# A two-block fp32 transformer kernel: token-tile entries with wide up and gate products, and pooling factors moved into the band matrix and the weights

## The chip, the cores and the metric

The kernel runs on one core of one Trainium2 chip. The metric is the device time of one execution in microseconds (us); less is better. Engines are named as in the profile: PE is TensorE's matmul stream, PEld its weight loads, DVE is VectorE, ACT is ScalarE, POOL is GpSimd, SP is SyncE, which issues the weight transfers.

## What is computed

Two blocks of two layers each on 256 tokens of width 1024, all in float32. Block one: causal attention, a squared-ReLU MLP, a pooling mixer, a second MLP. Block two: latent attention, a SwiGLU layer (called ffn here), shared keys and values, chunked attention, a second ffn. The parts that the change touches, cut from the reference:

```python
def pool_mixer(xn, w_groups, ls_scale):
    ...                      # per group: trailing mean over 2, 4, 8 or 16 tokens, minus the token
    y = jnp.einsum('bsgc,gcd->bsgd', pooled.astype(xn.dtype), w_groups)
    return y.reshape(b, s, D_MODEL) * ls_scale

def squared_relu_mlp(x, w_up, w_down):
    h = jax.nn.relu(x @ w_up)
    return (h * h) @ w_down

def swiglu(h, w_gate, w_up, w_down):
    return (jax.nn.silu(h @ w_gate) * (h @ w_up)) @ w_down

# second block, each layer
x = x + rms_norm_2(y, attn_post_g[layer])
h = rms_norm_2(x, ffn_pre_g[layer])
f = swiglu(h, ffn_w_gate[layer], ffn_w_up[layer], ffn_w_down[layer])
x = x + rms_norm_2(f, ffn_post_g[layer])
```

## The kernel before

**Numbers in two parts.** A float32 operand is used as a high part (rounded to the fast matmul format fp32r) plus a low part (the rest). `product` makes each matrix product from three matmuls into the same sums: high by high, low by high, high by low. Weights come in 1 MB chunks `raw[slot]` of 128 x 2048, four slots; ACT writes the high part `whi` (`hi_part`, L611), DVE the low part `wlo` (`lo_part`, L964), in the order of the chunk list, and PE waits for a chunk with `wait_chunk`. SP refills `raw` once the low part is made. `hi_before(c)` and `lo_before(c)` put into ACT's and DVE's queues the parts of all chunks whose slot is free before chunk c.

**Up and gate chunks.** `tiles_out` takes a chunk of 1024 x 256 weights as stationary 128 x 128 tiles and streams the 256 tokens of `act_hi` or `act_lo`: 2 output tiles x 8 input tiles x 3 matmuls of 256 columns, 48 in all. In an MLP ACT then takes the ReLU, DVE squares (L1210), ACT makes `hhi`, DVE `hlo`. In an ffn DVE scales the gate by the token's norm (L1238), ACT takes silu, DVE multiplies by the up product (L1246). The two MLPs have 16 up chunks each, the two ffns 11 gate and 11 up chunks each; the key part of the shared keys and values has 4 chunks of the same shape.

**Down chunks.** `rows_out` keeps token tiles stationary and streams 512 weight columns: 24 matmuls into four banks, one for each quarter (half of the width, token tile). PE's order is up(i+1), down(i), so the hidden tile i has one up chunk (an ffn: a gate and an up chunk) of time to be made ready.

**Entries.** Between two layers the sums in the four banks become the next layer's input. In block two `post` does this on DVE: ACT sums squares of a whole token tile from the banks (L642), DVE multiplies by the gain row (L1118), makes the inverse root with five small steps, adds to `x` in halves (L1122) and multiplies by the next gain (L1076). PE transposes the four quarters (`turn`, L1608), ACT and DVE make `act_hi` (L664) and `act_lo` (L1091), and the first gate chunk starts when the four parts are there. The norm itself is not yet in this input: its factor for each token is made meanwhile (`stats`, `diagonals`), spread by a small matmul (`spread_scales`) and multiplied in by L1238. These entries are called post0 (into ffn0), fpost0 (into the shared keys) and post1 (into ffn1). `keep_busy` puts dummy matmuls of a constant (L1592) into waits of PE, by the table `BUSY`.

**The pooling entry.** After MLP 0 `residual` adds the quarters to `x` (L1103), `norm("mix1")` waits for ACT's sums over both token tiles and scales `x` by factor and gain (L1031), PE multiplies with the banded matrix `const` (L1898, L1900; `C_BAND`) in plain float32, ACT and DVE split the result (L1349), PE multiplies with the pool weights (L1570 to L1572), and for each quarter DVE multiplies by the row `pool_scale` (L1357), adds to `x` (L1358) and multiplies by the next gain (L1076). Then the transposes, and MLP 1.

**POOL** loads the gain rows (three row slots, freed in turn by DVE) and scales the bias tables of the last attention (L501).

## Time and profile before

| what | value |
|---|---|
| median of 3 runs | 1159.61 us (1159.13 to 1159.83) |
| the profiled execution: its own time | 1158.01 us |
| its span in the trace | 1156.2 us |
| PE busy | 1113.8 us, 96% of the span, 7094 matmuls |
| DVE busy | 676.5 us, 59% |
| ACT busy | 532.0 us, 46% |
| POOL busy | 43.1 us, 4% |
| mean TensorE clock granted | 0.995 of full speed |
| chain that ended last | PE 85%, DVE 9%, ACT 3% |
| transfers | 196.36 MB, mean 170 GB/s |

The time of one run is what the runs are compared by; the span leaves out 1.8 us around it. A matmul's duration in the trace holds its latency, so two that follow each other overlap: what a stream of matmuls costs is read from the distance of their starts. Times within the trace are counted from the start of the span.

### The profile page before, as it was taken

The page shows a single profiled execution, that of the slowest core. Times are in us where ns is not written, and L with a number is a line of the kernel's source. Part 1 is how long each engine was busy: PE and PEld are TensorE (multiplying, and loading weights), DVE is VectorE, ACT ScalarE, POOL GpSimd, SP SyncE. Part 2 cuts the span into 40 slices and gives each one's busy share as a digit, 9 for nine tenths or more (in the row PEclk, how much of TensorE's full clock was granted, in tenths as well). Part 3 has the DMA queues.
Part 4 walks back from the last instruction along what each step waited for, and adds up shares of the span by engine and source line. Part 5 has one row for each costly group of instructions (what it writes and reads, how often), then busy time and mean ns, then how long its engine had stood idle before and what let it go on. Part 6 is the DMA issues. An engine that isn't in the chain of part 4 may idle for free.

```text
span 1156.2 us, 17758 instructions
## 1 busy us (share of the span) xinstructions
PE 1113.8 (96%) x7094; PEld 996.7 (86%) x7094; DVE 676.5 (59%) x941; ACT 532.0 (46%) x645; POOL 43.1 (4%) x71
## 2 busy tenths in 40 slices
PE   7999999999999999998999999999999979999997
PEld 6888899999889999988777999999798759999996
DVE  5756645454665454576667555454955766555554
ACT  5556434434344444345474433434534654334342
POOL 1000000000000000000000000001500410000000
PEclk9999999999999999999999999999999999999999
DMA  9843465555534555554432655556565143555650
GB/s 344 316 147 109 130 214 165 200 183 179 196 108 159 205 178 185 192 135 165 146 110 73 212 188 175 188 181 223 173 218 169 43 132 111 182 183 180 186 177 36
DMA packets 127273, 196.36 MB, mean 170 GB/s; under 512 B 6960, under 2 KB 97200, under 8 KB 127104
## 3 DMA queue, kind: packets, MB, share of 16 engines
q1 hardware_dynamic: 123872, 185.77, 49.0%
q0 software_dynamic: 3216, 9.51, 2.8%
q8 instruction: 27, 0.44, 0.2%
q10 hardware_dynamic: 144, 0.52, 0.1%
q14 instruction: 14, 0.11, 0.0%
HBM read 194.73 MB, written 1.05 MB: 169 GB/s over the span
## 4 chain that ended last, share of the span: by engine, by line
PE 85%; DVE 9%; ACT 3%; issue 1%; DMA 1%; DVEq 0%; SPq 0%; ACTq 0%
PE ps L1570 27%; PE ps L1572 26%; PE ps L1571 26%; DVE wlo L964 2%; DVE xs L1076 1%; ACT whi L611 1%; PE ps L1686 1%; DVE act_lo L1091 1%; DVE x L1122 1%; PE ps L2020 1%; DVE xs L1118 1%; DMA x<-x_in 1%; ACT junk L642 1%; PE ps L2018 1%; PE ps L1712 1%
## 5 line engine op out<-in xcount | busy, mean ns | idle before, releaser
L964 DVE TENSOR_TENSOR wlo<-raw,whi 128x2048 fp32r<-128x2048 f32 (+2 forms) x172 | 386.6, 2266 | 171.2 <-ACT whi L611 170.4
L1570 PE MATMUL ps<-act_hi,whi 128*128 128x256 f32 x1384 | 392.7, 284 | 6.2 <-DVE act_lo L1091 4.0
L1571 PE MATMUL ps<-act_lo,whi 128*128 128x256 f32 x1384 | 391.6, 283 | 0.0
L1572 PE MATMUL ps<-act_hi,wlo 128*128 128x256 f32 x1384 | 391.6, 283 | 0.0
L611 ACT ACTIVATE whi<-raw 128x2048 fp32r<-128x2048 f32 (+2 forms) x171 | 319.5, 1888 | 95.6 <-PE ps L1572 92.0
L1570 PEld LDWEIGHTS ps<-act_hi,whi 128*128 128x128 f32 x1384 | 263.6, 190 | 11.4 <-issue 7.6
L1571 PEld LDWEIGHTS ps<-act_lo,whi 128*128 128x128 f32 x1384 | 263.6, 190 | 2.0
L1572 PEld LDWEIGHTS ps<-act_hi,wlo 128*128 128x128 f32 x1384 | 263.6, 190 | 0.0
L1572 PE MATMUL ps<-whi,hlo 128*128 128x512 f32 x400 | 156.8, 392 | 0.0
L1571 PE MATMUL ps<-wlo,hhi 128*128 128x512 f32 x400 | 156.8, 392 | 0.0
L1570 PE MATMUL ps<-whi,hhi 128*128 128x512 f32 x400 | 156.2, 390 | 0.0
L1570 PE MATMUL ps<-whi,act_hi 128*128 128x512 f32 (+2 forms) x286 | 111.4, 390 | 5.8 <-DVE act_lo L1167 2.5
L1572 PE MATMUL ps<-whi,act_lo 128*128 128x512 f32 (+2 forms) x286 | 107.9, 377 | 0.0
L1571 PE MATMUL ps<-wlo,act_hi 128*128 128x512 f32 (+2 forms) x286 | 107.5, 376 | 0.0
L1210 DVE TENSOR_TENSOR arena<-arena 128x512 f32<-128x512 f32 x32 | 22.1, 692 | 129.1 <-ACT arena L721 129.1
L721 ACT ACTIVATE arena<-ps 128x512 f32<-128x512 f32 x32 | 19.1, 598 | 153.8 <-PE ps L1572 153.8
L1572 PEld LDWEIGHTS ps<-whi,hlo 128*128 128x128 f32 x400 | 75.2, 188 | 16.0
L1570 PEld LDWEIGHTS ps<-whi,hhi 128*128 128x128 f32 x400 | 75.2, 188 | 14.7
L1571 PEld LDWEIGHTS ps<-wlo,hhi 128*128 128x128 f32 x400 | 75.1, 188 | 14.6
L1570 PEld LDWEIGHTS ps<-whi,act_hi 128*128 128x128 f32 x286 | 53.8, 188 | 15.3 <-DVE act_lo L1167 3.2
L1572 PEld LDWEIGHTS ps<-whi,act_lo 128*128 128x128 f32 x286 | 53.7, 188 | 9.8
L1571 PEld LDWEIGHTS ps<-wlo,act_hi 128*128 128x128 f32 x286 | 53.9, 189 | 8.1
(186 smaller groups left out, 873.0 us busy)
## 6 DMA issues: line engine op xcount, KB each, us to landing
raw<-mlp_w_up_in SPq DMA_DIRECT2D x32, 1024.0 KB, 6.4
raw<-mlp_w_down_in SPq DMA_DIRECT2D x32, 1024.0 KB, 4.9
raw<-ffn_w_gate_in SPq DMA_DIRECT2D x22, 1024.0 KB, 5.3
raw<-ffn_w_up_in SPq DMA_DIRECT2D x22, 1024.0 KB, 5.3
raw<-ffn_w_down_in SPq DMA_DIRECT2D x22, 1024.0 KB, 4.8
raw<-attn_w_qkv_in SPq DMA_DIRECT2D x11, 1024.0 KB, 10.9
raw<-w_kv_shared_in SPq DMA_DIRECT2D x8, 1024.0 KB, 6.4
raw<-attn_w_o_in SPq DMA_DIRECT2D x4, 1024.0 KB, 5.1
```

The source lines that it names most:

```text
L611: nc.scalar.activation(whi[:, s, 0:width], raw[:, s, 0:width], ACT.Copy).then_inc(hi_ready, 1)
L642: nc.scalar.activation(junk[:, col * HALF:col * HALF + width], src, ACT.Square, accum_out=norm_stat(name, t, 0, col, col + 1)).then_inc(sq ...
L721: nc.scalar.activation(relu, bank(5 if first else 4), ACT.Relu).then_inc(f.act_done, 1)
L964: nc.vector.tensor_tensor(wlo[:, s, 0:width], raw[:, s, 0:width], whi[:, s, 0:width].bitcast(F32), ALU.subtract).then_inc(lo_ready, 1)
L1076: nc.vector.tensor_tensor(xs[:, t, cols], x[:, t, cols], row(name)[:, cols], ALU.mult)\
L1091: nc.vector.tensor_tensor(act_quarter(act_lo, name, p), bank(4 + p).rearrange("p (k t) -> p k t", t=P), act_quarter(act_hi, name, p).bitca ...
L1118: nc.vector.tensor_tensor(xs[:, t, :], ps[:, t * D:(t + 1) * D], row(name), ALU.mult)
L1122: nc.vector.scalar_tensor_tensor(out=x[:, t, cols], in0=xs[:, t, cols], scalar=norm_stat(name, t, 6), in1=x[:, t, cols], op0=ALU.mult, op1 ...
L1210: nc.vector.tensor_tensor(hf, relu, relu, ALU.mult).then_inc(f.h_done, 1)
L1570: nc.tensor.matmul(dst, lhsT=left[0], rhs=right[0], start=start, stop=False, **kw)
L1571: nc.tensor.matmul(dst, lhsT=left[0], rhs=right[1], start=False, stop=False, **kw)
L1572: return nc.tensor.matmul(dst, lhsT=left[1], rhs=right[0], start=False, stop=stop, **kw)
```

## The change

**Wide products.** `act_hi` and `act_lo` become the two halves of one tile `act`, so that for each 128-row piece the 256 high and 256 low columns lie side by side. `wide_out` replaces `tiles_out` for all up, gate and shared-key chunks: one matmul streams 512 columns against the high weights, and one of 256 columns streams the high activations against the low weights, 32 matmuls for a chunk instead of 48. The high-by-high and low-by-high sums now lie apart in a bank, and each chunk takes two banks; ACT copies the low half out (`copy_rest`), DVE adds the other half (`sum_gate`, `sum_up`, the first step of `square`). ReLU and square are one DVE instruction.

**Entries by token tiles.** At post0, fpost0 and post1 `post_entry` takes the place of `post`. POOL multiplies `x` and the two gain rows ahead of time (`premix_x`, `premix_rows`; 9 instructions of 128 x 1024); DVE makes the next input directly from the banks, token tile 0 before token tile 1; `enter_by_tiles` makes the first chunk's products of tile 0 before tile 1 is transposed. `x` itself is brought up to date later by `update_x`, between the layer's first steps. The dummy matmuls of these entries are gone.

**Pooling.** The token factor of `mix1` goes into the band matrix (`band`, scaled by ACT for token tile 0 and by DVE for tile 1), `pool_scale` into the pool weights (`scale_pool_weights`, one DVE instruction of 128 x 2048 during the last steps of MLP 0). The sums of squares are taken in quarters, MLP 0 ends tile by tile, and the 15 dummy matmuls before the band products and 8 of the 11 after them are gone.

```diff
-                    "fpre0": (4, 1, 6, 1, 2), "kvsrc": (8, 1, 6, 1, 2), 
-                    "fpre1": (4, 1, 6, 1, 2),
...
+            def wide_out(w, b, enter=None):
...
+                        nc.tensor.matmul(bank(b + f), lhsT=w[0][:, at:at + P],
+                                         rhs=act[:, k, :, :].rearrange("p a t -> p (a t)"),
+                                         start=k == 0, stop=False, skip_group_check=True)
+                        ins = nc.tensor.matmul(bank(b + f, 0, T), lhsT=w[1][:, at:at + P], rhs=act_hi[:, k, :],
+                                               start=False, stop=k == KT - 1, skip_group_check=True)
...
+            def enter_by_tiles(name, w, b):
+                turn(name, parts=(0, 1))
+                for t in range(TT):
+                    for kh in range(2):
+                        wait_acts(name, 2 * t + kh + 1)
...
+                                nc.tensor.matmul(both, lhsT=w[0][:, at:at + P], rhs=act[:, k, :, t * P:(t + 1) * P],
+                                                 start=k == 0, stop=False, skip_group_check=True)
+                                ins = nc.tensor.matmul(main, lhsT=w[1][:, at:at + P],
...
+                    if t == 0:
+                        turn(name, parts=(2, 3))
...
                 def gate_up(c, i, value, first=False, spread=False):
...
                     if first:
+                        enter_by_tiles(norm, slot(c), GATE).then_inc(w_used, 1)
+                    else:
+                        pe.wait_ge(f.summed, i * 2 - 1)
+                        wide_out(slot(c), GATE).then_inc(w_used, 1)
...
+                def copy_rest(value, b):
+                    act.wait_ge(w_used, value)
+                    nc.scalar.activation(by_token(up_sum), wide(b)[1], ACT.Copy).then_inc(f.rest_copied, 1)
...
+                    nc.vector.tensor_tensor(by_token(up_sum), wide(b)[0], by_token(up_sum), ALU.add)\
+                        .then_inc(f.summed, 1)
+                    dve.wait_ge(f.summed, i + 1)
+                    nc.vector.scalar_tensor_tensor(out=hf, in0=up_sum, scalar=0.0, in1=up_sum, op0=ALU.max,
+                                                   op1=ALU.mult).then_inc(f.h_done, 1)
...
-            keep_busy(15, 7)
...
+                pe.wait_ge(band_second if t else band_first, 1)
```

DVE's queue at post0, before: from the first statistics of token tile 0 (`stat`) to the low parts of the input.

```order
L1001 TENSOR_SCALAR stat<-stat 128x1
L1118 TENSOR_TENSOR xs<-ps,rows 128x1024
L1017 RECIPROCAL stat<-stat 128x1
...
L1122 SCALAR_TENSOR_TENSOR x<-xs,stat,x 128x512
L1076 TENSOR_TENSOR xs<-x,rows 128x512
L1122 SCALAR_TENSOR_TENSOR x<-xs,stat,x 128x512
L1076 TENSOR_TENSOR xs<-x,rows 128x512
```

This stands twice, once for each token tile, and then come all four low parts. In the changed kernel the same place reads as follows for tile 1 and behind it.

```order
L1238 TENSOR_SCALAR stat<-stat 128x1
L1234 TENSOR_TENSOR arena<-ps,xs 128x512
L1243 SCALAR_TENSOR_TENSOR stat<-stat 128x1
L1198 TENSOR_TENSOR act<-ps,act 128x4x128
L1234 TENSOR_TENSOR arena<-ps,xs 128x512
...
L1198 TENSOR_TENSOR act<-ps,act 128x4x128
L1262 SCALAR_TENSOR_TENSOR xs<-arena,stat 128x512 x2
L1198 TENSOR_TENSOR act<-ps,act 128x4x128 x2
L1071 TENSOR_TENSOR wlo<-raw,whi 128x2048
L1290 TENSOR_TENSOR arena<-ps,rows 128x512 x2
L1294 SCALAR_TENSOR_TENSOR x<-arena,stat,x 128x512 x2
```

The low parts of tile 0 (the first two L1198) moved ahead of tile 1's input (L1262), and the update of `x` (L1290, L1294) moved behind all four.

PE's queue in an up chunk, before, three matmuls of 256 columns for each pair of tiles:

```order
L1570 MATMUL ps<-act_hi,whi 128x256
L1571 MATMUL ps<-act_lo,whi 128x256
L1572 MATMUL ps<-act_hi,wlo 128x256
L1570 MATMUL ps<-act_hi,whi 128x256
L1571 MATMUL ps<-act_lo,whi 128x256
```

The same chunk in the changed kernel, here the first of MLP 1:

```order
L1925 MATMUL ps<-act,whi 128x512
L1928 MATMUL ps<-act,wlo 128x256
L1925 MATMUL ps<-act,whi 128x512
L1928 MATMUL ps<-act,wlo 128x256
L1925 MATMUL ps<-act,whi 128x512
```

One matmul in three is gone, the columns streamed are the same.

## Rows read from the trace of the kernel before

**Rows 1.** The page: busy time by engine, then its costliest group of products.

```profile
PE 1113.8 (96%) x7094; PEld 996.7 (86%) x7094; DVE 676.5 (59%) x941; ACT 532.0 (46%) x645; POOL 43.1 (4%) x71
...
L1570 PE MATMUL ps<-act_hi,whi 128*128 128x256 f32 x1384 | 392.7, 284 | 6.2 <-DVE act_lo L1091 4.0
```

**Rows 2.** Timeline, PE, ffn0: start, duration, engine, line, operation; chunks' first matmuls.

```profile
695.68 0.29 PE L1570 MATMUL ps<-act_hi,whi 128*128 128x256 f32 x1
...
701.44 0.40 PE L1570 MATMUL ps<-whi,hhi 128*128 128x512 f32 x1
...
706.95 0.28 PE L1570 MATMUL ps<-act_hi,whi 128*128 128x256 f32 x1
```

**Rows 3.** Timeline, PE: 16 transposes of 128 columns in a row.

```profile
872.98 1.91 PE L1608 MATMUL ps<-const,xs 128*128 128x128 f32 x16
```

**Rows 4.** Timeline, PE, post0: last product, transposes, first product, first down chunk.

```profile
614.25 0.39 PE L1572 MATMUL ps<-whi,act_lo 128*128 128x512 f32 x1
...
618.30 0.66 PE L1608 MATMUL ps<-const,xs 128*128 128x128 f32 x4 [1.94 <-DVE xs L1076]
...
626.87 0.36 PE L1570 MATMUL ps<-act_hi,whi 128*128 128x256 f32 x1
...
650.41 0.39 PE L1570 MATMUL ps<-whi,hhi 128*128 128x512 f32 x1
```

**Rows 5.** Timeline, DVE, from post0's first multiplication to the down chunk's low part.

```profile
614.60 1.22 DVE L1118 TENSOR_TENSOR xs<-ps,rows 128x1024 f32<-128x1024 f32 x1
...
616.70 0.75 DVE L1122 SCALAR_TENSOR_TENSOR x<-xs,stat,x 128x512 f32<-128x512 f32 x1
...
624.84 2.48 DVE L1091 TENSOR_TENSOR act_lo<-ps,act_hi 128x512 fp32r<-128x512 f32 x4 [0.26 <-DVE xs L1076]
...
642.34 2.29 DVE L964 TENSOR_TENSOR wlo<-raw,whi 128x2048 fp32r<-128x2048 f32 x1 [1.11 <-ACT whi L611]
```

**Rows 6.** Groups by line over the whole span: ACT's copies and DVE's square.

```profile
L1210 DVE TENSOR_TENSOR arena<-arena 128x512 f32<-128x512 f32 x32 | 22.1, 692 | 129.1 <-ACT arena L721 129.1
...
L664 ACT ACTIVATE act_hi<-ps 128x512 fp32r<-128x512 f32 x32 | 18.5, 596 | 45.7 <-PE ps L1608 45.7
```

**Rows 7.** Timeline, fpost0: PE's last and first product, DVE's low parts before it.

```profile
808.46 6.69 DVE L964 TENSOR_TENSOR wlo<-raw,whi 128x2048 fp32r<-128x2048 f32 x3 [2.63 <-ACT whi L611]
...
814.27 0.40 PE L1572 MATMUL ps<-whi,last_hlo 128*128 128x512 f32 x1
...
827.64 0.36 PE L1570 MATMUL ps<-act_hi,whi 128*128 128x256 f32 x1 [0.72 <-DVE act_lo L1091]
```

**Rows 8.** Timeline, post1: PE's last product, DVE's first statistics, PE's first product.

```profile
945.15 0.39 PE L1572 MATMUL ps<-whi,act_lo 128*128 128x512 f32 x1
...
947.80 0.15 DVE L1001 TENSOR_SCALAR stat<-stat 128x1 f32<-128x1 f32 x1 [4.21 <-ACT junk L642]
...
960.14 0.36 PE L1570 MATMUL ps<-act_hi,whi 128*128 128x256 f32 x1 [0.72 <-DVE act_lo L1091]
```

**Rows 9.** Timeline, pooling: MLP 0's last matmul, DVE's low part, pool and MLP 1 starts.

```profile
306.30 0.39 PE L1572 MATMUL ps<-whi,last_hlo 128*128 128x512 f32 x1
...
319.00 0.36 PE L1570 MATMUL ps<-whi,act_hi 128*128 128x256 f32 x1
...
321.71 2.29 DVE L964 TENSOR_TENSOR wlo<-raw,whi 128x2048 fp32r<-128x2048 f32 x1 [1.11 <-ACT whi L611]
...
333.99 0.36 PE L1570 MATMUL ps<-act_hi,whi 128*128 128x256 f32 x1 [0.55 <-DVE act_lo L1091]
```

**Rows 10.** Windows: busy by engine, PEclk is the granted clock, then transfer share, GB/s.

```profile
616.73:620.14 3.41, 1.55 (x10) 1.15 (x11) 3.27 (x6) 0.41 (x2) 0.00 (x0) 1.00 0.00 0
620.15:623.55 3.40, 3.40 (x10) 2.77 (x9) 3.19 (x9) 0.87 (x2) 0.00 (x0) 0.50 0.02 5
```

**Rows 11.** Timeline, POOL's bias scaling and four DVE multiplications beside it.

```profile
826.92 8.37 POOL L501 TENSOR_SCALAR arena<-arena 128x256 f32<-128x256 f32 x8
831.58 2.88 DVE L1076 TENSOR_TENSOR xs<-x,rows 128x512 f32<-128x512 f32 x4
```

More of the change, by code:

```diff
@@ L337, in act_quarter, with wide @@
             return acts[:, 4 * h:4 * h + 4, t * P:(t + 1) * P]
+        def wide(b):
+            both = ps[:, b * HALF:(b + 2) * HALF].rearrange("p (f a t) -> p f a t", a=2, t=T)
+            return both[:, :, 0, :], both[:, :, 1, :]
         def by_token(ap):
@@ L553, in _, with premix_x, premix_rows @@
             pool.wait_ge(hi_ready, 2)
-            for name in ROWS[1:ROW["pre1"] + 1]:
-                load_row(name)
+            def premix_x(then):
+                for t in range(TT):
+                    nc.gpsimd.tensor_tensor(x_gained[then][:, t, :], x[:, t, :], row(then), ALU.mult)\
+                        .then_inc(premixed, 1)
+            def premix_rows(name, then):
+                nc.gpsimd.tensor_tensor(both_rows[then], row(name), row(then), ALU.mult).then_inc(premixed, 1)
+            for name in ROWS[1:ROW["fpost0"] + 1]:
+                load_row(name)
+            wait_row(pool, "post0")
+            wait_row(pool, "fpre0")
+            pool.wait_ge(qr_turned, 2)
+            pool.wait_ge(x_scaled, 2)
+            premix_x("fpre0")
+            pool.wait_ge(mla.mixed, 8)
+            premix_rows("post0", "fpre0")
+            load_row("kvsrc")
+            load_row("pre1")
+            wait_row(pool, "fpost0")
+            wait_row(pool, "kvsrc")
+            pool.wait_ge(x_ready, 4 * XR["fpre0"] + 4)
+            pool.wait_ge(turned, 4 * TURN["fpre0"] + 4)
+            premix_x("kvsrc")
+            premix_rows("fpost0", "kvsrc")
             pool.wait_ge(ffn[0].lo_done, NF)
@@ L567, in _, with split_stats @@
                 scale_bias(pool, h)
-            load_row("fpost1")
+            wait_row(pool, "post1")
+            wait_row(pool, "fpre1")
+            pool.wait_ge(turned, 4 * TURN["pre1"] + 4)
+            premix_x("fpre1")
+            pool.wait_ge(chk.scored, KT)
+            premix_rows("post1", "fpre1")
+            load_row("fpost1")
+        def split_stats(act, sum_squares, root, name, done, acc):
+            for t in range(TT):
+                for h in range(2):
+                    p = 2 * t + h
+                    act.wait_ge(*((acc_part, 3 * acc + p + 1) if p < 3 else (w_used, done)))
+                    if p >= 2:
+                        act.wait_ge(squares, squares_before(name) + p - 1)
+                    sum_squares(name, t, bank(p), HALF, h)
+                root(name, t)
         def post_stats(act, sum_squares, root, name, done, acc):
@@ L715, in mlp_layer @@
                 n0 = f.first
-                def head(i, first):
-                    act.wait_ge(w_used, n0 + 1 if first else i * 2 + n0)
-                    if not first:
-                        act.wait_ge(f.h_done, i)
-                    nc.scalar.activation(relu, bank(5 if first else 4), ACT.Relu).then_inc(f.act_done, 1)
                 def tail(i, first, last=False):
@@ new lines, in update_x @@
+            def update_x(name, t):
+                if t == 0:
+                    wait_row(dve, name)
+                for h in range(2):
+                    cols = slice(h * HALF, (h + 1) * HALF)
+                    ins = nc.vector.tensor_tensor(y_gained[:, t, cols], bank(2 * t + h), row(name)[:, cols], ALU.mult)
+                link(ins)
+                for h in range(2):
+                    cols = slice(h * HALF, (h + 1) * HALF)
+                    nc.vector.scalar_tensor_tensor(out=x[:, t, cols], in0=y_gained[:, t, cols],
+                                                   scalar=norm_stat(name, t, 6), in1=x[:, t, cols],
+                                                   op0=ALU.mult, op1=ALU.add).then_inc(x_ready, 1)
+                if t == TT - 1:
+                    dve.sem_inc(row_used, 2)
@@ L1342, in _, with scale_pool_weights @@
             late_roots("mlp0", square=True)
-            mlp_layer(mlp[0])
+            def scale_pool_weights():
+                c = AT["pool"]
+                wait_row(dve, "pool_scale")
+                dve.wait_ge(w_loaded[SLOT[c]], 16 * NTH[c])
+                w = raw[:, SLOT[c], :].rearrange("p (g k f) -> p g k f", g=4, k=2)
+                by_channel = row("pool_scale").rearrange("p (g f) -> p g f", g=4).unsqueeze(2)
+                nc.vector.tensor_tensor(w, w, by_channel.broadcast_to([P, 4, 2, FC]), ALU.mult)\
+                    .then_inc(pool_weighted, 1)
@@ L1352, in _ @@
             lo_before(AT["pool"])
-            wait_row(dve, "pool_scale")
             for p in range(4):
@@ L1776, in down @@
                     rows_out(slot(c), 0, lambda k, t: (hi[:, k, t * P:(t + 1) * P], lo[:, k, t * P:(t + 1) * P]),
-                             first, last, QUARTERS if last else None).then_inc(w_used, 1)
-                up(n0, 0, n0 + 1, True)
-                up(n0 + 1, 1, n0 + 2, second=True)
+                             first, last, final if last else None).then_inc(w_used, 1)
+                up(n0, 0, n0 + 1, 4, early=True)
+                up(n0 + 1, 1, n0 + 2, 6, early=True)
                 down(n0 + 2, 0, n0 + 3, first=True)
```

416 lines of the change are left out of this document (295 added, 121 removed).

## The prediction

> **What bounds the kernel now.** First the page's busy times, then the chain that ended last, then the timeline. PE is busy for 1113.8 of 1156.2 us [rows 1], so time can only be won where PE streams less or waits less. The trap is in the costliest group: its 1384 matmuls have a mean of 284 ns [rows 1], and two such groups more would be over the whole span, so these durations overlap. The price of a matmul is the distance of two starts. An up chunk of 48 matmuls of 256 columns runs from 695.68 to 701.44, 0.120 us each; a down chunk of 24 matmuls of 512 columns runs from 701.44 to 706.95, 0.2296 us each [rows 2]. That is about 0.107 and 0.213 us of columns at the 2.4 GHz level and 13 to 16 ns that each matmul adds. So a matmul that is left out while its columns stay is worth some 10 ns, not 284.
>
> The rest lies at the entries. I call E the moment at which PE has streamed the last product before an entry. At post0 E is 614.48 (the last start and its 0.23 us) and the first product starts at 626.87, E+12.4 [rows 4]; at fpost0 E is 814.50 and the start 827.64, E+13.1 [rows 7]; at post1 945.38 and 960.14, E+14.8 [rows 8]; at the pooling 306.53, pool products at E+12.5, MLP 1 at E+27.5 [rows 9]. These are 68 us of entries (the 5.8 us of pool products among them), during most of which PE runs dummies: they count as busy and the page does not show them as waits.
>
> **Wide products.** For each pair of tiles three matmuls of 0.120 us (0.360) become one of 512 and one of 256 columns (0.2296 + 0.120 = 0.350). 32 MLP up chunks, 42 of the 44 gate and up chunks of the ffns and 3 of the 4 key chunks take this form: 77 x 16 pairs x 10.4 ns = **12.8 us**. All of it is on the path if the new steps behind the products stay hidden. In an MLP step the hidden tile now needs a copy (0.6, the length of L664), an add (0.7), the fused square (0.75), the high part (0.6) and the low part (0.69), with two weight parts of 2.29 in DVE's queue [rows 5, 6]: 8.0 us, against a down and an up chunk, 5.5 + 5.6 = 11.1. In an ffn step the add stands before the scaling and silu, and the next gate's weights follow in both queues: about 6.9 us of 11.1. Hidden, with 3 us or more to spare; DVE's load of 10.3 us in an ffn step of 16.7 is no bound.
>
> TensorE: Matmul & The Clock Gate, of the Trainium skill, gives in "Back-to-back issue gap" N/2.4 + 2.5 ns for matmuls in a row. By that, each dropped matmul would return 2.5 ns and the wide form 3.1 us in all. The starts above show 13 ns and more beside the columns, so the trace disagrees.
>
> **post0 by token tiles.** Tile 0's two banks are full 1.4 us before E, and ACT now sums each half as it comes, so both sums are there at E-0.4. DVE: two half multiplications of 0.61 (half of 1.22), four small steps at 0.2, two input halves at 0.7: E+2.8. Then tile 1's first multiplication and statistics, 1.0; ACT's root, one copy of 0.6, DVE's low part 0.7: PE starts products at **E+5.3** instead of E+12.4. But they are half size: for tile 0, 16 x (a matmul of 2 x 128 columns + one of 128). The first is a 256-column matmul, 0.120. For the second no fp32r row exists. The nearest below is the columns alone plus the fixed part, 0.067; 16 plain fp32 transposes of 128 columns take 1.91 us, 0.109 each [rows 3]; above stands one twice as dear, 0.21. I take 0.109, the same weights and columns. A tile costs 3.7 us, the chunk 7.3 instead of 5.8. Second piece of tile 0 at E+7.4 (DVE: 0.6, 0.8, 0.7 in between), transposes of tile 1 at E+9.3, copy, low part, tile 1 from E+11.0: first chunk done at E+14.7, where it was E+18.2.
>
> What is late next is the first down chunk, at 650.41 = E+35.9 before, with its low weight part made by 644.63, 5.8 us early [rows 4, 5]. PE would be there at 14.7 + three chunks of 5.6 + 0.4 for the spread = E+31.9. DVE now has, before that low part, two updates of `x` (2.7 each), two adds (0.7), and two weight parts (2.3); following its queue, the low part is ready at E+32.7, or E+33.7 if POOL is in its way. So the entry's gain is cut by DVE to about 3, and 0.5 of it is the wide form already counted.
>
> **The clock.** The dummies go. In the window 616.73 to 620.14 PE was busy for 1.55 of 3.41 us, and the next 3.4 us ran at 0.50, the 1.2 GHz level [rows 10]. That fell on dummies and cost nothing. After the change PE does 0.9 us of transposes between E and E+5.3, less than in that window, so I expect the lower level at each of the three entries, now over products: 3.4 us at half speed lose **1.7 us** each. For post0 this gives PE E+33.6, DVE E+33.7: gain 35.9 - 33.7 - 0.5 = **1.7 us**.
>
> **post1** starts 3.1 us later in its chain (ACT makes half a weight part first, DVE began at 947.80, E+2.4 [rows 8]): first chunk done at E+17.8, first down chunk at 17.8 + 16.8 + 0.4 + 1.7 = E+36.7. Before, it came four chunks and the spread (4 x 5.76 + 0.4 = 23.4 us, as at post0) behind 960.14, at E+38.2: gain **1.0**. **fpost0**: DVE's three low parts end at 815.15, E+0.6 [rows 7]; they start 1.4 later now, since copy and add lengthen the last hidden tile. First chunk done at E+17.9, with the clock E+19.6, before E+19.0: **-0.6**. Later key chunks have their sums in time.
>
> **Pooling.** To the pool products it is a draw: DVE is free at E+0.6 because of its low parts, then two adds, two gains, statistics, band factor for tile 0 at E+5.9, for tile 1 at E+9.8, and the products start at E+12.2 (E+12.4 with the band matmuls at the lower clock) against 12.5. Behind them DVE still makes a low part of 2.29 first (321.71 before [rows 9]), done at E+16.9, and then takes 1.4 instead of 2.1 us for each quarter (the gain of `pool_scale` is gone): MLP 1 from E+24.0 instead of E+27.5. With the clock 1.1 back: **2.4 us**. `scale_pool_weights`, 2.3 us on DVE, lies in DVE's wait for the next up chunk: 129.1 us in 32 such waits, 4.0 each [rows 6].
>
> **POOL.** Nine multiplications of 128 x 1024 are new; no row shows their price. Between DVE's 1.2 us for 1024 columns and four of POOL's eight steps of 256 columns (8.37 us for 8, so 4.2) I take 2.5. Six of them lie long before they are needed; post0's gain rows can start only when the last head is mixed, two times 12 matmuls of 512 columns before E, E-5.5. They would be done at E-3.0, at the dear end at E-1.3, and are wanted at E-1.1; setting up POOL's first one could cost 1 or 2 us more. Beside POOL's steps four DVE multiplications took 2.88 us where they take 2.5 [rows 11]. I charge 0.8 us in all. SBUF — State Buffer, of the Trainium skill, says in its table on the engines' ports that a DVE instruction with two SBUF inputs and a POOL one that reads SBUF block each other for a whole instruction. By that DVE could lose up to the 22 us of POOL's work, nearly all where it has slack; the row shows a delay of 0.4 us, less than one instruction.
>
> **Sum.** 12.8 + 1.7 + 1.0 - 0.6 + 2.4 - 0.8 = **16.5 us**. The profiled execution took 1158.0, so 1141.5; the median of the runs is 1.6 above it, so 1143.1.
>
> **The rivals.**
> (a) The clock stays up and the half-size matmuls cost 0.067: 3 x 1.7 + 1.1 and 3 x 1.0 back, no POOL cost, less 1 us that DVE keeps at post0: 9 us, 1134. For it: fpost0 kept its clock before. Against: it had 16 dummies in a row.
> (b) The entries give nothing or take: half-size rest matmuls at 0.21 (96 x 0.1 = 10 us), or DVE's queue late by 2 us at each entry: only the wide form is left, less a few us, 1148 to 1154. For it: DVE already sets post0.
> (c) The fixed part of a matmul belongs to loading weights and vanishes in the wide form (a weight load of 190 ns now has 348 ns for two instead of 240): 335 ns a pair, another 18 us: 1125. Against: the down chunks have the same room and pay 16 ns.
> (d) The wide form does not do what it says, because its 512-column matmul is dearer by those 10 ns: 1156.
> (e) Slower: the copy and the add do not hide. The place is the wait for the hidden tile's low part in front of a down chunk; each us by which it comes too late costs 30 us in the 30 looped MLP steps. It decides from 0.6 us per step (16.5 + 2.3 over 30), and I have 3.1 us of room; with 1 us late the time would be 1172.
>
> **How the numbers follow.** Forecast 0.50, (a) 0.18, (b) 0.18, (c) 0.05, (d) 0.04, (e) 0.05. The range takes in (a) and most of (b): 1134 to 1152. What a measurement of this kernel can tell from no change is about 0.2%, 2.3 us. Slower by more: 0.04, from (e); within: 0.03, the edges of (d) and (e); faster: 0.93.
>
> **What would show it.** Starts 0.35 us apart from pair to pair in up and gate chunks, and no PE wait in the loops (else e). At post0 the first product at E+5 to 6 and the first down chunk near E+33.5; PEclk 0.50 for some 3.4 us right behind each of the three entries (else a); the 128-column matmuls 0.11 behind their start (0.07: a, 0.21: b). MLP 1 starts 25 us after MLP 0's end. I am wrong if the wide pairs take under 0.34 or over 0.36, or if an entry's first down chunk comes later than before.

## The result, and the profile after

The changed kernel takes 1165.83 us (median of 5, 1163.83 to 1168.34), the kernel before 1159.61: a ratio of 1.0048, 95% interval 1.0033 to 1.0063. It is 6.2 us slower where 16.5 us less were forecast. The profiled execution took 1165.83 us, its span is 1164.0 against 1156.2, and its mean granted clock 0.977 against 0.995.

The page of the changed kernel, the rows that answer to [rows 1]: busy times, clock by slices, and the wide half of a pair.

```profile
PE 1094.6 (94%) x5772; PEld 923.4 (79%) x5772; DVE 749.4 (64%) x1043; ACT 558.4 (48%) x711; POOL 68.7 (6%) x80
...
PEclk9999999999899999999998899999899988999999
...
L1925 PE MATMUL ps<-act,whi 128*128 128x512 f32 x1232 | 437.8, 399 | 1.7 <-DVE act L1198 0.9
```

PE is busy for 19.2 us less and the span is 7.8 us longer: PE waits more. Its waits in the changed kernel (what it waited for: us in total, times, longest):

```profile
PE ps L1872 <- DVE xs L1262: 12.8, 3, 5.8
PE ps L1944 <- DVE act L1198: 6.6, 6, 1.6
PE ps L1986 <- DVE probs L1349: 6.5, 3, 3.8
PE ps L2199 <- ACT arena L925: 5.9, 1, 5.9
...
PE ps L1958 <- DVE probs L1158: 4.4, 1, 4.4
```

Three of these lines (L1872, L1944 and L2199) are the entries, where dummies had run. The other two are stalls: in the attentions (L1986, where the kernel before waits once, for 1.5 us) and in ffn0's first steps (L1958), which is new. None lies in a loop.

A table by stage, from starts of PE (E as before; "down" is the first down chunk):

| stage | before | changed |
|---|---|---|
| start to the first product of MLP 0 | 126.5 | 127.8 |
| MLP 0, MLP 1, each | 180.1 | 178.4 |
| pooling, end of MLP 0 to MLP 1 | 27.5 | 25.0 |
| latent attention, to post0's E | 100.4 | 102.2 |
| post0, E to down | 35.9 | **41.5** |
| rest of ffn0 | 164.1 | 162.0 |
| fpost0's E to post1's E | 130.9 | **137.7** |
| post1, E to down | 38.3 | 39.7 |
| rest of ffn1 | 164.1 | 162.9 |

Pooling does what was forecast (in two later profiles of the same code there it took 26.1 us). The losses are behind post0 and between fpost0 and post1.

**The stall in ffn0.** Timeline of the changed kernel: DVE's small steps for the spread, POOL's premixed products, then PE (start, duration, engine, line):

```profile
637.05 0.17 DVE L1127 TENSOR_SCALAR stat<-stat 128x2 f32<-128x2 f32 x1
637.25 2.28 DVE L1135 TENSOR_TENSOR stat<-stat 128x2 f32<-128x2 f32 x1
639.57 2.28 DVE L1154 TENSOR_TENSOR stat<-stat 128x2 f32<-128x2 f32 x1
641.88 2.27 DVE L1156 TENSOR_SCALAR stat<-stat 128x2 f32<-128x2 f32 x1
...
637.13 4.70 POOL L584 TENSOR_TENSOR xs<-x,rows 128x1024 f32<-128x1024 f32 x2 [3.25 <-DMA rows<-kv_src_g_in]
641.79 2.33 POOL L589 TENSOR_TENSOR arena<-rows 128x1024 f32<-128x1024 f32 x1
...
644.68 1.19 PE L1958 MATMUL ps<-probs,const 128*128 128x128 f32 x4 [4.41 <-DVE probs L1158]
...
653.30 0.50 PE L1836 MATMUL ps<-whi,hhi 128*128 128x512 f32 x1
```

Steps on two numbers a partition take 2.28 us, with one POOL product beside each. L1127, a step of the same size just ahead of POOL's first product, takes 0.17.

The same in the chunked attention, DVE's softmax steps, POOL, PE:

```profile
936.91 1.76 DVE L1337 TENSOR_SCALAR soft<-soft 128x2 f32<-128x2 f32 x1
...
939.91 2.46 DVE L1349 TENSOR_SCALAR probs<-probs,soft 128x128 f32<-128x128 f32 x2
...
942.48 0.55 DVE L1349 TENSOR_SCALAR probs<-probs,soft 128x128 f32<-128x128 f32 x2
...
938.61 3.41 POOL L589 TENSOR_TENSOR arena<-rows 128x1024 f32<-128x1024 f32 x1
...
942.43 0.55 PE L1986 MATMUL ps<-const,probs 128*128 128x128 f32 x3 [3.77 <-DVE probs L1349]
```

Two L1349 take 2.46 us beside POOL and 0.55 a moment later.

**The clock.** Windows of the changed kernel (busy by engine, then the granted clock): post0, ffn0 behind the stall, fpost0, post1.

```profile
615.83:619.24 3.41, 2.47 (x11) 2.47 (x12) 3.08 (x8) 2.45 (x3) 0.00 (x0) 0.50 0.00 0
619.24:622.65 3.41, 3.41 (x17) 3.41 (x17) 0.83 (x2) 0.00 (x0) 0.00 (x0) 0.51 0.00 0
...
646.50:649.91 3.41, 3.41 (x12) 2.86 (x11) 1.95 (x3) 2.06 (x3) 0.00 (x0) 0.50 0.00 0
...
825.70:830.82 5.12, 5.12 (x26) 5.12 (x26) 1.86 (x3) 0.01 (x1) 0.00 (x0) 0.50 0.20 71
...
962.23:967.35 5.12, 5.12 (x25) 5.12 (x25) 2.08 (x4) 0.00 (x0) 0.00 (x0) 0.50 0.00 0
```

PE streams products in all of them at 0.50, the 1.2 GHz level. In [rows 10] one stretch of 3.4 us lay on dummies. Now the stretches last 6.8 us at the pooling, at post0 and in ffn0, 10.2 us at fpost0 and at post1, and 3.4 us in the chunked attention. Not all of that lies on products: at the pooling the first 3.7 us, at fpost0 and post1 the first 3.6 and 3.9 us pass before PE's first product.

### The profile page after: what moved, and what is told of

Read it like the earlier page. It is cut to its first block, busy times and chain, and to the rows that moved or that the text cites. A ratio compares the mean times of both kernels' runs of the same rounds, so it can differ in the third digit from the quotient of the medians.

```text
span 1164.0 us, 15260 instructions
## 1 busy us (share of the span) xinstructions
PE 1094.6 (94%) x5772; PEld 923.4 (79%) x5772; DVE 749.4 (64%) x1043; ACT 558.4 (48%) x711; POOL 68.7 (6%) x80
## 4 chain that ended last, share of the span: by engine, by line
PE 80%; DVE 12%; ACT 5%; issue 2%; DMA 1%; DVEq 0%; ACTq 0%; SPq 0%
PE ps L1925 23%; PE ps L1836 13%; PE ps L1838 12%; PE ps L1837 12%; PE ps L1928 12%; DVE wlo L1071 3%; ACT whi L680 2%; PE ps L1944 2%; DVE act L1198 1%; PE ps L1986 1%; DVE xs L1183 1%; PE ps L2319 1%; DMA x<-x_in 1%; PE ps L2317 1%; PE ps L2012 1%
## 5 line engine op out<-in xcount | busy, mean ns | idle before, releaser
L1925 PE MATMUL ps<-act,whi 128*128 128x512 f32 x1232 | 437.8, 399 | 1.7 <-DVE act L1198 0.9
L1928 PE MATMUL ps<-act,wlo 128*128 128x256 f32 x1232 | 346.1, 281 | 0.0
L680 ACT ACTIVATE whi<-raw 128x2048 fp32r<-128x2048 f32 (+2 forms) x171 | 319.3, 1887 | 34.6 <-PE ps L1838 25.4
L1925 PEld LDWEIGHTS ps<-act,whi 128*128 128x128 f32 x1232 | 232.3, 189 | 58.9 <-issue 3.3
L1928 PEld LDWEIGHTS ps<-act,wlo 128*128 128x128 f32 x1232 | 233.6, 190 | 1.9
L1836 PE MATMUL ps<-whi,act 128*128 128x512 f32 (+2 forms) x286 | 112.7, 394 | 6.1 <-DVE wlo L1485 2.0
L1838 PE MATMUL ps<-whi,act 128*128 128x512 f32 (+2 forms) x286 | 109.0, 381 | 0.0
L1837 PE MATMUL ps<-wlo,act 128*128 128x512 f32 (+2 forms) x286 | 108.6, 380 | 0.0
L799 ACT ACTIVATE arena<-ps 128x512 f32<-128x512 f32 x32 | 19.2, 600 | 148.7 <-PE ps L1928 148.7
L1836 PEld LDWEIGHTS ps<-whi,act 128*128 128x128 f32 x286 | 54.6, 191 | 16.0 <-issue 3.1
L1838 PEld LDWEIGHTS ps<-whi,act 128*128 128x128 f32 x286 | 54.3, 190 | 10.0
L824 ACT ACTIVATE arena<-ps 128x512 f32<-128x512 f32 x44 | 26.2, 594 | 74.9 <-PE ps L1928 66.5
L1837 PEld LDWEIGHTS ps<-wlo,act 128*128 128x128 f32 x286 | 54.7, 191 | 8.3
L1387 DVE TENSOR_TENSOR hlo<-arena,hhi 128x512 fp32r<-128x512 f32 x50 | 34.4, 688 | 24.5 <-ACT hhi L836 23.1
```

Of the source, the lines that this page charges most:

```text
L680: nc.scalar.activation(whi[:, s, 0:width], raw[:, s, 0:width], ACT.Copy).then_inc(hi_ready, 1)
L799: nc.scalar.activation(by_token(up_sum), wide(b)[1], ACT.Copy).then_inc(f.rest_copied, 1)
L824: nc.scalar.activation(by_token(dst), wide(b)[1], ACT.Copy).then_inc(f.rest_copied, 1)
L1387: nc.vector.tensor_tensor(lo[:, :, :].rearrange("p k t -> p (k t)"), hf, hi[:, :, :].rearrange("p k t -> p (k t)").bitcast(F32), ALU.subtr ...
L1836: nc.tensor.matmul(dst, lhsT=left[0], rhs=right[0], start=start, stop=False, **kw)
L1837: nc.tensor.matmul(dst, lhsT=left[0], rhs=right[1], start=False, stop=False, **kw)
```

## The experiments

Theory: two things that the change brought along cost more than it won. POOL's products hold up DVE, one whole instruction at a time ("port"), and without dummies PE is given the 1.2 GHz level over products ("clock"). A third miss, smaller, is the price of a pair. Each run is the changed kernel with the edit shown, unless it says otherwise.

### The shared keys' products later

```diff
-            premix_x("kvsrc")
-            premix_rows("fpost0", "kvsrc")
+            for t in range(TT):
+                pool.wait_ge(ffn[0].lo_done, 3 + 2 * t)
+                nc.gpsimd.tensor_tensor(xs[:, t, :], x[:, t, :], row("kvsrc"), ALU.mult).then_inc(premixed, 1)
+            pool.wait_ge(ffn[0].lo_done, 7)
+            premix_rows("fpost0", "kvsrc")
```

> The changed kernel with one edit: POOL makes the three premixed products for the shared keys not in ffn0's first steps but inside ffn0's loop (behind its hidden tiles 3, 5 and 7). Port theory: three of DVE's five small steps of statistics took 2.28, 2.28 and 2.27 us instead of 0.16, one POOL instruction each, so the spread came 6.4 us late and PE stood still for 4.4 us and then ran 3.4 us at the 1.2 GHz level. Moved into the loop, where DVE waits several us in each step, they cost nothing: first down chunk at E+34.6 instead of E+41.5, no stretch at 0.50 in front of it, 6 to 7 us less than the changed kernel, about 1159. Queue theory (DVE's queue is late by itself, with two updates of x and two sums in front of the statistics, as the prediction had feared): DVE's instructions are the same in the same order, so E+41.5 and 1166.

Measured: 1161.36 us, 4.5 less; 6 to 7 were expected. DVE and PE in ffn0's first steps:

```profile
639.49 0.16 DVE L1138 TENSOR_TENSOR stat<-stat 128x2 f32<-128x2 f32 x1
...
639.89 0.17 DVE L1159 TENSOR_SCALAR stat<-stat 128x2 f32<-128x2 f32 x1
...
650.61 0.50 PE L1839 MATMUL ps<-whi,hhi 128*128 128x512 f32 x1 [1.89 <-DVE wlo L1074]
```

The first and the last of the three steps, 0.16 and 0.17: DVE's queue is unchanged, so the queue theory falls. The down chunk comes at E+36.9 and not E+34.6: PE now waits 1.9 us for the low weight part, which the prediction had named as next. So the port made 4.6 us of the delay, and behind it DVE's low part still sets the chunk.

### The same products in pieces

```diff
-            premix_x("kvsrc")
-            premix_rows("fpost0", "kvsrc")
+            for t in range(TT):
+                for q in range(4):
+                    cut = slice(q * 256, (q + 1) * 256)
+                    ins = nc.gpsimd.tensor_tensor(xs[:, t, cut], x[:, t, cut], row("kvsrc")[:, cut], ALU.mult)
+                ins.then_inc(premixed, 1)
...
```

> The changed kernel with the three POOL products for the shared keys cut into twelve of 256 columns, at the same place. Port theory, with the block lasting for one whole instruction: POOL works as long as before (7 us or somewhat more), but each of DVE's small steps is held for at most one short instruction, about 0.6 us, so that the three steps lose under 2 us instead of 6.4: first down chunk near E+36.5, time 1160 to 1162. If the block lasted as long as POOL has work at all, whatever the size of its instructions, the first down chunk would stay at E+41.5 or come later, 1166 or more. Queue theory: E+41.5, 1166.

Measured: 1164.47 us (by 1.4 us less, which the two sets of runs, 1161.99 to 1166.03 and 1163.83 to 1168.34, hardly part); down at E+38.3, a gain of 3.3 us there. DVE's steps:

```profile
640.63 0.60 DVE L1143 TENSOR_TENSOR stat<-stat 128x2 f32<-128x2 f32 x1
...
641.97 0.67 DVE L1164 TENSOR_SCALAR stat<-stat 128x2 f32<-128x2 f32 x1
642.54 1.53 DVE L1166 TENSOR_SCALAR probs<-const,stat 128x128 f32<-128x128 f32 x2
```

A step is held for one POOL instruction and no longer: 0.6 us beside 256 columns, 2.28 beside 1024. I had stopped counting after three steps. The twelve pieces last 9.4 us, and the steps behind the first three pay too (L1166: 1.53 instead of 0.47). Shorter instructions soften the block, only another time removes it.

### The width alone undone

```diff
-                        nc.tensor.matmul(bank(b + f), lhsT=w[0][:, at:at + P],
-                                         rhs=act[:, k, :, :].rearrange("p a t -> p (a t)"),
+                        nc.tensor.matmul(bank(b + f, 0, T), lhsT=w[0][:, at:at + P], rhs=act_hi[:, k, :],
+                                         start=k == 0, stop=False, skip_group_check=True)
+                        nc.tensor.matmul(bank(b + f, T, 2 * T), lhsT=w[0][:, at:at + P], rhs=act_lo[:, k, :],
...
```

This kernel leaves out a part of its sums (which part, and by what, was not traced); for PE the work is that of three matmuls for each pair.

> The changed kernel with the width alone undone: in each pair three matmuls of 256 columns again (96 for two chunks), sums, copies and adds as they are. The prediction's price, 10.4 ns a pair over 77 chunks of 16 pairs: 12.8 us slower than the changed kernel, 1178.6. The price read from the starts in the changed kernel (a pair at 0.347 to 0.356 us against 0.360): 0.06 to 0.2 us a chunk, 5 to 8 us slower, 1171 to 1174. If the issue gap were 2.5 ns a matmul: 3.1 us slower, 1169.

Measured: 1173.86 us, 8.0 more than the changed kernel. An MLP takes 180.1 us again, as before the change. So the width is worth 8.0 us, not 12.8 and not 3.1.

### Dummies back in the waits

```diff
+                keep_busy({"fpre0": 8, "kvsrc": 26, "fpre1": 22}[name], GATE)
                 turn(name, parts=(0, 1))
+                keep_busy(7, GATE)
...
+            keep_busy(26, 7)
             for t in range(TT):
                 lo, hi = ((0, T), (T, 3 * P))[t]
```

> The changed kernel with dummy matmuls back in PE's waits at the new entries (8, 26 and 22 of 256 columns before the transposes of post0, fpost0 and post1, 7 behind them; 26 before the band products). Clock theory: the stretches at 0.50 of 6.8, 6.8, 10.2 and 10.2 us at these four places lay over products and cost 1.6 (pooling), 2.9 (post0), 3.3 (fpost0) and 3.2 us (post1); with PE kept streaming they vanish: 11 us less, about 1155; the stretches in ffn0 and in the chunked attention, which are behind other stalls, stay. Rival: the level falls all the same, or the dummies end too late and hold up the transposes: within 2 us of 1166, or above.

Measured: 1176.4 us, 10.6 more, at a mean clock of 0.993. A miss of my own, and the trace says which. PE at fpost0:

```profile
820.84 11.38 PE L1856 MATMUL ps<-const 128*128 128x256 f32 x52
832.06 1.04 PE L1872 MATMUL ps<-const,xs 128*128 128x128 f32 x8
832.93 3.19 PE L1856 MATMUL ps<-const 128*128 128x256 f32 x14
```

26 dummies are 52 matmuls in the trace: one takes 0.43 us, and I had counted 0.22. They ran 5 us past what PE was waiting for. Half of each number was tried next:

> The changed kernel with half the dummies of the run before (one dummy took 0.43 us, twice what its count assumed): 4, 13 and 11 before the transposes of post0, fpost0 and post1, 3 behind them, 13 before the band products, so that they end 0.2 to 0.5 us before what PE waits for. Clock theory: no stretch at 0.50 at these four places, first products at E+5.0, E+8.7, E+8.0 as in the changed kernel, a tile of them in 3.8 instead of 6.4 to 6.7 us: 11 us less than the changed kernel, 1155. Rival: what the clock gives at the entries is taken back by the next wait, for DVE's low parts in front of the first down chunk: then only pooling and fpost0 keep it, 3 to 5 us, 1161 to 1163.

Measured: 1155.96 us, 9.9 less than the changed kernel (0.9971 of the kernel before, 0.9957 to 0.9984). PE at post0, and windows at fpost0 and post1:

```profile
614.27 1.89 PE L1856 MATMUL ps<-const 128*128 128x256 f32 x8
616.31 1.32 PE L1872 MATMUL ps<-const,xs 128*128 128x128 f32 x8 [0.16 <-DVE xs L1262]
617.47 1.46 PE L1856 MATMUL ps<-const 128*128 128x256 f32 x6
619.27 0.39 PE L1946 MATMUL ps<-act,whi 128*128 128x256 f32 x1 [0.35 <-DVE act L1198]
...
825.40:830.40 5.00, 3.99 (x35) 3.61 (x33) 3.02 (x6) 1.54 (x3) 0.00 (x0) 1.00 0.29 108
...
956.30:961.30 5.00, 4.59 (x30) 3.78 (x30) 4.07 (x12) 2.13 (x4) 0.00 (x0) 1.00 0.00 0
```

First products at E+5.0, 8.9 and 8.1, as in the changed kernel, now at 1.00. A tile of them takes 3.9 us with the way to the next transposes, where it took 6.4 to 6.8. At the pooling MLP 1 starts after 23.7 instead of 25.0 us (24.9 to 26.1 in the five profiles without these dummies). The stretch behind the stall in ffn0 stays, as expected.

### All nine products moved

Those for the shared keys as in the first run; the other six on DVE, which waits there for the last output products:

```diff
+            mix_x("fpre0")
+            mix_rows("post0", "fpre0")
             post_entry("post0")
...
+                if j == KT + 1:
...
+                    mix_x("fpre1")
                 split_out(chk, j - 2)
...
+            mix_rows("post1", "fpre1")
             post_entry("post1")
```

> The changed kernel with all nine premixed products away from the places where they hold DVE: those for the shared keys on POOL inside ffn0's loop, those for post0 and post1 on DVE itself (six instructions of 1.2 us), in its waits for the last output products. Port theory: besides the 4.6 us of the run with the shared keys' products alone, the latent attention gets its 1.8 us back and the chunked attention its 4.9 us (3.1 of stall and 1.7 of the 1.2 GHz level behind it); up to 1 us is lost where DVE's own six stick out: 1155 to 1157. Rival: DVE pays for its own 7.2 us as much as it lost to POOL: 1161, as with the shared keys' products alone.

Measured: 1156.09 us, 9.7 less than the changed kernel, and 3.3 less than the kernel before on the same chip. The latent attention takes 101.3 instead of 102.2 us, with a stretch of 3.4 us at the 1.2 GHz level in it that the changed kernel's profile has not. The first experiment, with that stretch and with POOL's products there, took 102.9: moving them gives 1.6 us back, of the 1.8 expected. From fpost0's E to post1's it takes 133.0 instead of 137.7. The down chunk of post0 comes at E+35.9 instead of E+41.5:

```profile
648.23 0.50 PE L1845 MATMUL ps<-whi,hhi 128*128 128x512 f32 x1 [1.78 <-DVE wlo L1061]
```

### Both edits

> Both edits: the nine products moved and the halved dummies. If port and clock are the two causes and do not overlap, the sum of the two gains: 10 + 11 us less than the changed kernel, 1145, which would also beat the kernel before by 1.2%. If they overlap (a shorter chain ends in a wait for the same low parts), 1149 to 1153.

Measured: 1146.92 us, 0.988 of the kernel before (0.986 to 0.9899) and 18.9 less than the changed kernel; the two gains, 9.7 and 9.9, add to within 0.7 us, less than the runs can tell. DVE in front of post0, then PE from E to the down chunk:

```profile
607.23 2.35 DVE L1753 TENSOR_TENSOR arena<-x,rows 128x1024 f32<-128x1024 f32 x2
609.50 1.22 DVE L1757 TENSOR_TENSOR xs<-rows 128x1024 f32<-128x1024 f32 x1
610.75 0.15 DVE L1228 TENSOR_SCALAR stat<-stat 128x1 f32<-128x1 f32 x1
...
611.74 1.89 PE L1865 MATMUL ps<-const 128*128 128x256 f32 x8
...
616.81 0.38 PE L1955 MATMUL ps<-act,whi 128*128 128x256 f32 x1 [0.35 <-DVE act L1188]
617.03 0.22 PE L1957 MATMUL ps<-act,wlo 128*128 128x128 f32 x1
617.09 0.33 PE L1955 MATMUL ps<-act,whi 128*128 128x256 f32 x1
617.26 0.22 PE L1957 MATMUL ps<-act,wlo 128*128 128x128 f32 x1
...
645.71 0.50 PE L1845 MATMUL ps<-whi,hhi 128*128 128x512 f32 x1 [1.87 <-DVE wlo L1061]
```

DVE makes the three products in 3.5 us (POOL took 7.2) and is done when the first sum comes. The down chunk starts at 645.71 = E+34.0, again behind DVE's low part: 1.9 us earlier than without dummies, and after the same wait. So the clock also delays what DVE waits for.

### The order of the wide matmuls

The kernel with both edits, and in it:

```diff
                                          start=k == 0, stop=False, skip_group_check=True)
+                    for k in range(KT):
+                        at = k * FC + f * P
                         ins = nc.tensor.matmul(bank(b + f, 0, T), lhsT=w[1][:, at:at + P], rhs=act_hi[:, k, :],
```

> The kernel with both edits (products moved, dummies back), and in each wide output tile first the eight matmuls of 512 columns, then the eight of 256, instead of in turn. Why the width brought 8 and not 12.8 us: in turn, the distances of two starts fall into one of two rhythms, 0.347 us a pair (0.230 and 0.117 at all times) or 0.3525 to 0.356 (0.232 to 0.241 and 0.113 to 0.120 by turns), mostly the second. Theory A, the price is one of each matmul whatever stands beside it, 0.2296 and 0.120: a chunk takes 5.59 us in either order and the run is at most 3 us faster than the kernel with both edits (1146.9), by the end of the slow rhythm: 1143.5 to 1147. Theory B, the change from one width to the other costs something by itself: two changes for eight pairs instead of sixteen, chunks at 5.55 or below, 4 us faster or more. Theory C, the 256-column matmuls pay for their own weight loads, which the wide neighbours cover now and which eight narrow ones in a row do not: chunks at 5.7, slower by 3 us or more.

Measured: 1144.72 us. The medians are 2.2 us apart, and the intervals (0.9844 to 0.9885, 0.986 to 0.9899) overlap; the trace is sharper. PE in MLP 0, one output tile of a chunk and the start of the next:

```profile
222.51 2.00 PE L1934 MATMUL ps<-act,whi 128*128 128x512 f32 x8
224.35 1.11 PE L1939 MATMUL ps<-act,wlo 128*128 128x256 f32 x8
225.30 2.00 PE L1934 MATMUL ps<-act,whi 128*128 128x512 f32 x8
```

A tile is 2.79 us (222.51 to 225.30), a pair 0.349: the price of theory A. Theories B and C, with chunks at 5.55 and 5.7, fall: two tiles are 5.58. An MLP takes 177.5 us instead of 178.4, so a chunk gains 0.161 us on the kernel before, where the prediction had 0.167 and the changed kernel 0.105.

### Two dummies in the latent attention

The kernel with both edits and `keep_busy(2, 6)` behind the transposes of `qr_tok`.

> The kernel with both edits and two dummies more (0.86 us), in the latent attention behind the transposes of the rotated queries, where PE waits 0.9 to 1.2 us. In four of the five profiles of edited kernels a stretch of 3.4 or 6.8 us at the 1.2 GHz level began 3 to 4 us behind this wait, over products, in none of the two unedited ones. If that wait is what sets it off: no stretch between 545 and 570, 1 to 2.5 us faster than the kernel with both edits, 1144.5 to 1146. If it comes from waits further ahead: the stretch stays and the time too, 1147.

Measured: 1144.97 us, and no stretch between 545 and 570. But the grouped kernel, without these dummies, had none either. The count in the expectation does not hold: all seven profiles of edited kernels before this run had a stretch in the latent attention, three (6.8 us, from 559.6, 560.5 and 561.2) 3 us behind this wait, and four (3.4 us, from 546.7 to 550.3) about 13 us ahead of it, behind another wait of 1.6 us for a low weight part. The changed kernel had none. Dummies at this place can bear on the first kind alone, and the kernel with all edits, which has them, shows the second kind at 541.8. So the cause stays open, and the 2 us against the kernel with both edits are no proof: that one's profile had a stretch of 6.8 us here, and the intervals overlap.

### The kernel before without its dummies

```diff
-                    "fpre0": (4, 1, 6, 1, 2), "kvsrc": (8, 1, 6, 1, 2), 
-                    "fpre1": (4, 1, 6, 1, 2),
...
-            keep_busy(15, 7)
```

> The kernel before with its dummy matmuls taken out at post0, fpost0, post1 and in front of the band products, and nothing else: that part of the change alone. Clock theory: first products at the same E+12.4, 13.1, 14.8 and band products at E+7.2, but at the 1.2 GHz level for 3 to 7 us at each of the four places: 8 to 12 us slower, 1168 to 1172. Rival: the dummies of the kernel before did nothing for the clock (they had one stretch of 3.4 us on them at post0 and one at post1): 1159.6, or a little less where they had held up a transpose.

Measured: 1168.17 us, 7.6 more than the kernel before on the same chip (1160.56). Windows around post0's first product, at 632.94:

```profile
625.55:630.55 5.00, 2.23 (x8) 1.43 (x8) 4.76 (x12) 1.37 (x4) 0.00 (x0) 0.50 0.00 0
630.55:635.55 5.00, 3.72 (x16) 3.35 (x17) 2.93 (x8) 3.73 (x8) 1.05 (x2) 0.50 0.65 193
```

First products come at E+12.4, 13.1 and 14.8 as before, but at 0.50. The stretches are longer than expected: 10.2 us at the pooling, 13.7, 17.1 and 13.7 at the other three. The pooling loses 3.0 us, post0 1.7, fpost0 to post1's E 2.8, post1 1.8: 9.3 in this profile, of the slowest of the four runs. So the dummies were worth 7.6 us in the old entries, and 9.9 in the new ones; the intervals (1.0039 to 1.0075 here) do not part the two.

### All of it

Both edits, the grouped order and the two dummies.

> The kernel with both edits (products moved, halved dummies), the grouped order of the wide matmuls and the two dummies in the latent attention. If the order is worth the 0.9 us in each MLP and 0.4 us in an ffn that its trace showed, and the two dummies keep the latent attention from its stretch at the 1.2 GHz level (which the grouped kernel's profile did not have either, so that this is open), the two do not add: 1143 to 1145. If both add fully to the kernel with both edits: 1142.8.

Measured: 1142.66 us, 0.9849 of the kernel before (0.9829 to 0.9868): the lowest median of all, though its interval overlaps those of the last two. Whether the two edits add, the runs cannot tell.

## Why the prediction was wrong

Forecast and measurement lie 22.7 us apart. POOL makes 8.9 of it, the wide products 4.8, the clock 3.7, or 5.4 since its 1.7 us at post0 never entered the sum (see below); 3.6 to 5.3 us are left. With its mis-sized POOL term alone put right, the forecast would still have been 7.6 us less, so the sign needed more than one miss. But POOL's is the largest, and either cure alone, the products moved or the dummies back, puts the kernel 3.3 to 3.4 us ahead of the one before.

**POOL, charged with 0.8 us: measured 9.7**, the 1.2 GHz stretches behind its stalls among them. This is the step that failed. It took "a delay of 0.4 us, less than one instruction" from [rows 11], and "nearly all where it has slack" from nothing but the order. That row sums four DVE and eight POOL instructions, and hides who waited: there POOL's steps are short (256 columns, one operand) and it was partly POOL that was held. Taken one by one, two of its POOL steps took 1.37 and 1.33 us and the other six 0.85 to 0.87, two of its DVE steps 0.88 and the other two 0.67 and 0.68. A single pair of the changed kernel shows it, DVE's low part and POOL's bias scaling beside it, then the same scaling alone:

```profile
899.77 2.29 DVE L1071 TENSOR_TENSOR wlo<-raw,whi 128x2048 fp32r<-128x2048 f32 x1
...
901.27 1.50 POOL L528 TENSOR_SCALAR arena<-arena 128x256 f32<-128x256 f32 x1 [3.82 <-DMA arena<-b_rel_table_in]
...
906.16 0.84 POOL L528 TENSOR_SCALAR arena<-arena 128x256 f32<-128x256 f32 x1 [2.23 <-DMA arena<-b_rel_table_in]
```

POOL's step takes 0.7 us longer than alone; 0.8 were left of DVE's. The price of the nine products themselves was right: 2.4 us each against an assumed 2.5. Wrong was that only their own length mattered. SBUF — State Buffer, of the Trainium skill, in "SBUF: two separate sides", says that of a GpSimd instruction and a DVE one with two SBUF inputs the one that starts first has the port to itself and "the other fully blocks". By that rule, the trace agrees: 2.28 us for a step of 0.16 (L1135) that began 0.1 us behind POOL's. The prediction cited it, priced it at up to 22 us, and let the row decide; it should have been a rival with its places, since the order showed POOL's products beside the statistics chain.

**The clock, charged with 1.7 us an entry and 1.1 at the pooling, 6.2 in all: measured 9.9.** The mechanism was right, and the place: 0.50 at each entry, over products. The length was not: it was taken from the one stretch of [rows 10], 3.4 us between dummies, and in the new entries, where PE stands still for 2 to 6 us first, it is 6.8 and 10.2, of which 3.2 (pooling) and 5.9 to 6.6 us (the others) lie behind the first product. And dropping the dummies was a choice of the change that the prediction took as given. It read them as costing nothing; the two experiments show what they are worth.

**Wide products, 12.8 us: measured 8.0.** The additive price, 0.2296 + 0.120, holds for matmuls of one width in a row (grouped: 0.349 a pair). In turn, nearly all chunks of the MLPs and the loop of ffn1 ran at 0.352 to 0.353 a pair; ffn0 changed between 0.353 and 0.347 from step to step. The term was mis-sized by a row of another order. The gap of 2.5 ns that the Trainium skill gives for an isolated matmul (TensorE: Matmul & The Clock Gate, "Back-to-back issue gap") would make it 3.1 us as an estimate, as far off on the other side. The copy and the add stayed hidden, as forecast: no wait in the loops, so rival (e) did not come.

**post0.** First product at E+5.0 (forecast 5.3), right. The down chunk at E+41.5 instead of 33.7; in the kernel with both edits at E+34.0. The limit named, DVE's low part, is the one that is there once the port is out of the way: a wait of 1.87 us. But the prediction let the clock vanish there: PE at E+33.6 with it, beside a DVE at E+33.7 that did not depend on it. The runs show it on top. With the products moved the chunk comes at E+35.9 without dummies and at E+34.0 with them, after waits of 1.8 and 1.9 us for the same low part. So this overlap failed, and without dummies the entry gains nothing (E+35.9 before).

**post1.** First product at E+8.1 (forecast 5.3 + 3.1), right; down at E+39.7 instead of 36.7, with both edits 37.2. **fpost0.** First product at E+8.9, first chunk done at E+21.5 (forecast 19.6). DVE's three low parts end at 817.85, E+2.6; the prediction had put them at about E+2. Between fpost0's and post1's E 6.8 us were lost, of which both edits give back 7.4.

**Pooling.** MLP 1 at 25.0 us (forecast 25.1), right, with 26.1 in two other profiles, and 23.7 with the dummies (forecast 24.0). **The half-size matmuls**: the rest matmul's own distance is 0.06 (617.03 to 617.09), rival (a)'s price, but the 256 columns beside it take 0.17 (617.09 to 617.26) and not 0.120. A pair is 0.23, the sum that the prediction used (0.120 + 0.109), and a tile 3.7 us as forecast: the sum right, its two parts not, which is luck.

**The rivals.** None of them is what happened; (a) and (b) moved an entry by a few us, and the slower side had only (e), whose wait never came. The way in which an instruction off the path stretches one on it was not among them.

The sum of the prediction without its charges for POOL and clock is 22.5 us (23.5 less the 1 us that DVE keeps at post0, as in rival (a)); the fastest version is 17.1 us ahead of the kernel before, measured beside it. Part of what is missing may be PE's waits for DVE's low weight parts in front of down chunks, 6.0 us in 4 waits (longest 1.9) in the kernel with both edits against 2.2 in 2 before; the rest was not traced. The start of the kernel, the same in all, ranged from 126.2 to 129.5 us in the profiles, so the 1.3 us there is no effect of the change.

## What to carry to other kernels

Work that is given to POOL is not off DVE's path: ask for each POOL instruction which short DVE steps run beside it, and charge up to a whole instruction of POOL to each. Put it beside long slack or in DVE's own waits, where DVE did it in half the time. A wait for DVE does not hide a delay of PE where DVE's queue waits for PE itself: the low part that sets post0's chunk came 1.9 us later with the lower clock. Where an entry gets shorter, keep PE streaming in what is left of its waits, with dummies that end just before what it waits for, and read what one dummy takes in the trace first. A price made of two rows holds in the order in which those rows were measured.

## What the runs showed of the hardware

- A DVE instruction on two elements a partition took 2.28 us beside a POOL product of 1024 columns and 0.60 to 0.67 beside one of 256. Held were also steps of one SBUF tensor with a constant (L1156, 2.27 us beside 1024 columns) or with a scalar from SBUF (two L1349, 2.46 instead of 0.55 us), but not those that read PSUM (L1332 beside POOL's L584, 0.28 us for 128 columns, as without POOL).
- Matmuls of 512 and 256 columns in turn run in one of two rhythms, 0.347 or about 0.3525 us a pair, and keep it at least for a chunk or a gate and up chunk. The loop of ffn1 ran in one of them for all of its steps in the changed kernel (11.18 us for 64 matmuls) and by turns in others (10.98 and 11.17), as ffn0's did in the changed kernel. What chooses is open.
- Of the 1.2 GHz level: the kernels with dummies of the right length had none between E and the first chunk of an entry. Some had one of 3.4 us right behind PE's wait of 1.9 us in front of the first down chunk (from 971.2 with the grouped order, 972.3 with the two dummies, 640.8 with all edits). In the latent attention a stretch of 3.4 or 6.8 us came in some profiles and not in others, of kernels that are the same there.
